# One dependent chain for the 31 taps of a depthwise convolution, in a two-layer decoder step on one Trainium2 core

## The chip, the cores and the metric

The kernel runs on one core of a Trainium2 chip. The metric is the device time of one execution, in microseconds (us); lower is better. The core's engines run side by side and meet only at semaphores: TensorE (PE in the profile) multiplies matrices, VectorE (DVE) and ScalarE (ACT) work element by element and can read and write PSUM, GpSimd (POOL) works element by element in SBUF, SyncE (SP) issues most of the DMAs.

## The reference

Two layers over a residual stream of width 2048. A prompt of 1024 rows and 64 sample rows (8 sequences of 8) share the weights. Layer 0 is the part that the change touches:

```python
def conv_mixer(u, buf, w_in, conv_w, conv_b, ln_g, ln_b, w_out):
    z = u @ w_in
    a, b, gate = jnp.split(z, 3, axis=-1)
    c = a * jax.nn.sigmoid(b)
    full = jnp.concatenate([buf, c], axis=1)          # 30 earlier rows, then c
    y = depthwise_conv(full, conv_w)                  # 31 taps for each of 2048 features
    y = y + conv_b
    y = jax.nn.silu(layer_norm(y, ln_g, ln_b))
    out = (y * jax.nn.silu(gate)) @ w_out
```

For the prompt the 30 earlier rows are zeros; the samples bring theirs in `state_conv`. Layer 1 is a sliding-window attention with a gate. Each layer is `h = h + rms_norm(mixer(rms_norm(h)))`. All is float32.

## The kernel before, in words

Features lie on the 128 partitions, the 1088 rows (1024 of the prompt, 64 of the samples) on the free axis. A weight tile `n` gives 128 output features: PE goes over 16 slices `k` of the inputs and three column chunks of 364, 364 and 360, with three matmuls each, since weights and activations are held as a high and a low part (`w_hi`, `w_lo`, `u_hi`, `u_lo`). Tiles with an even number go to the PSUM tensor `z_even`, the odd ones to `z_odd`. For each quarter of a weight tile SP loads `w_raw`, ACT makes `w_hi` (L734, `split_w`), POOL makes `w_lo` (L1021, `rest_w`), and PE waits for it.

The convolution stage is a loop over 16 feature tiles `j`. Tile `2j` is the sigmoid's half, tile `2j+1` the other. For each `j`:

- DVE reads `z_odd` (L1302 to L1307), multiplied with the sigmoid, into `cp` (1024 prompt columns behind 30 zeros) and `cs` (samples).
- ACT writes tap 0 with the convolution's bias into `aux1` (L778), a PSUM tensor of two banks, and signals `tap0_ready`.
- DVE adds the other taps. Each is one `scalar_tensor_tensor` over 128x1024: a shifted window of `cp`, times one column of `cols`, plus the accumulator. After tap 15 it reads the next `z_even` (L1269, `read_z`).
- DVE signals `conv_ready`; ACT reads `aux1` out (`read_conv`, L762 to L765: a copy and a square), and after that, in its program order, makes the last quarter of a `w_hi` (L734) and the next tap 0 (L778).
- POOL adds the two results to the layer norm's sums (`add_y`, L1071 and L1072), and does the samples' whole convolution (L1094, L1102, L1106) between the first two and the last two quarters of `w_lo` of tile `2j+3`.

`j` = 0 and `j` = 15 are written out with constants; `j` = 1 to 14 are a hardware loop on DVE, where the value that a wait compares with, and the address of the tap's column in `cols`, are worked out by register instructions on the engine's queue (DVEq, and ACTq for ACT). In the program each tap has its wait on `tap` first and the instruction with its column's address behind it.

After `j` = 15 PE sums the layer norm's totals (L562) and goes on with gates, output projection, keys and values, attention and the last projection, none of which the change touches.

The accumulators before are two: `aux1` for the even taps, and `odd_taps` in SBUF for the odd ones. A tap waits only for the one two places back (`i - 2`), the one that last wrote its accumulator. `aux1` and `odd_taps` are added at the end (L1324).

Of the kernel before, what the change touches and what calls it, by code (L numbers as in the profile page):

```python
# [31 lines left out]
ALU = mybir.AluOpType  # L32
# [6 lines left out]
TP = 1024  # L39
SB, SS = 8, 8  # L40
TS = SB * SS
T = TP + TS
# [4 lines left out]
CW = 31  # L47
HIST = CW - 1
SEG = HIST + SS
# [11 lines left out]
C_CW = 128  # L61
# [28 lines left out]
def trunk_kernel(nc, x_t, state_t, ck_t, cv, w, cols_in, y_t, scp_t, ckp_t, cvp, scs_t, cks_t, cvs):  # L90
    ctx = ExitStack()
    with ctx:
        def sb(name, shape, dt=F32):
            return ctx.enter_context(nc.sbuf_tensor(name, shape, dt))

        def sem(name):
            return ctx.enter_context(nc.semaphore(name))
# [15 lines left out]
        cols = sb("cols", [P, NCOLS])  # L113
# [11 lines left out]
        aux1 = aux[:, :, :].rearrange("p a b -> p (a b)")  # L125

        def region(at, n):
            return work[:, at:at + n]

        def places(*sizes):  # L130
            out, at = [], 0
            for n in sizes:
                out.append(region(at, n))
                at += n
            assert at <= WORK, at
            return out


        (r_a, sig, y_st, y_sq, acc_y, acc_y2, cp, cs_flat, ys, prod, odd_taps) = places(
            T, T, T, T, T, T, TP + 32, SB * SEG, TS, 4 * SS * CW, TP)  # L140
        cs = cs_flat.rearrange("p (b s) -> p b s", b=SB)

        s_st = [region(8 * T, T), region(9 * T, T), region(T, T), region(3 * T, T)]
# [81 lines left out]
        conv_ready = sem("conv_ready")  # L225
        tap = sem("tap")
# [51 lines left out]
        def ge(eng, s, v):  # L278

            if not (isinstance(v, int) and v <= 0):  # L280
                eng.wait_ge(s, v)

        def chunk(ap, c):
            return ap[:, CHUNKS[c][0]:CHUNKS[c][0] + CHUNKS[c][1]]
# [962 lines left out]
        def _(dve):  # L1247
# [17 lines left out]
            def read_z(n, z, out, by):  # L1265

                dve.wait_ge(w_used, NQ * (n + 1))
                for c in range(3):
                    ins = dve.tensor_tensor(chunk(out, c), z[:, c, 0:CHUNKS[c][1]], chunk(by, c), ALU.mult)  # L1269
                ins.then_inc(z_read, 1)  # L1270
# [8 lines left out]
            for k in range(KT):  # L1279
                dve.wait_ge(u_hi_ready, k + 1)  # L1280
                dve.scalar_tensor_tensor(out=u_lo[:, k, :], in0=x_st[k % 4],
                                         scalar=cols[:, C_PRE0 + k:C_PRE0 + k + 1],
                                         in1=u_hi[:, k, :].bitcast(F32), op0=ALU.mult, op1=ALU.subtract
# [10 lines left out]
            def glu(j, nxt):  # L1294

                dve.wait_ge(w_used, NQ * (2 * j + 2))
                dve.wait_ge(sigr_ready, j + 1)
                ge(dve, ys_ready, j)
                ge(dve, state_out, 32 * j)
                ge(dve, conv_ready, j)  # L1300
                n0, n1 = CHUNKS[0][1], CHUNKS[1][1]
                dve.tensor_tensor(cp[:, HIST:HIST + n0], z_odd[:, 0, 0:n0], chunk(sig, 0), ALU.mult)  # L1302
                dve.tensor_tensor(cp[:, HIST + n0:HIST + n0 + n1], z_odd[:, 1, 0:n1], chunk(sig, 1), ALU.mult)
                left = TP - n0 - n1
                dve.tensor_tensor(cp[:, HIST + n0 + n1:HIST + TP], z_odd[:, 2, 0:left],
                                  sig[:, n0 + n1:TP], ALU.mult)
                dve.tensor_tensor(cs[:, :, HIST:SEG], z_odd[:, 2, left:left + TS].rearrange("p (b t) -> p b t", b=SB),  # L1307
                                  sig[:, TP:T].rearrange("p (b t) -> p b t", b=SB), ALU.mult).then_inc(z_read, 1)

                dve.wait_ge(z_read, 2 * j + 2)  # L1310
                dve.tensor_scalar(odd_taps, cp[:, 1:1 + TP], cols[:, bass.ds(C_CW + j * CW + 1, 1)], None,
                                  ALU.mult).then_inc(tap, 1)
                dve.wait_ge(tap0_ready, j + 1)
                for i in range(2, CW):
                    if i > 2:
                        dve.wait_ge(tap, (CW - 1) * j + i - 2)
                    acc = odd_taps if i % 2 else aux1
                    dve.scalar_tensor_tensor(out=acc, in0=cp[:, i:i + TP],  # L1318
                                             scalar=cols[:, bass.ds(C_CW + j * CW + i, 1)], in1=acc,
                                             op0=ALU.mult, op1=ALU.add).then_inc(tap, 1)  # L1320
                    if i == CW // 2 and nxt:
                        read_z(2 * j + 2, z_even, sig, r_a)
                dve.wait_ge(tap, (CW - 1) * j + CW - 1)
                dve.tensor_tensor(aux1, aux1, odd_taps, ALU.add).then_inc(conv_ready, 1)  # L1324

            glu(0, True)
            with dve.Fori(1, KT - 1) as j:
                glu(j, True)
            glu(KT - 1, False)


# [263 lines left out]
```

## Time and profile before

| | |
|---|---|
| median of 3 runs | 3283.92 us (3283.34 to 3286.16) |
| the profiled execution | 3287.02 us |
| its span in the trace | 3285.4 us |
| PE busy | 3081.3 us, 94% |
| DVE busy | 1505.7 us, 46% |
| POOL busy | 1551.2 us, 47% |
| ACT busy | 850.7 us, 26% |

Busy shares are means over the whole span. The convolution's loop takes the stretch from about 83 to 897 us, and there DVE is busy nearly all the time, while elsewhere it is busy for a third of the time or less. So what the change is worth has to be read from that stretch.

### The profile page before, as it was taken

The numbers are of one execution on the slowest core, as the hardware profiler recorded it, in microseconds if no ns is written. First come the engines' busy times: TensorE is split into PE (matmuls) and PEld (weight loads), VectorE is DVE, ScalarE is ACT, GpSimd is POOL, SyncE is SP. The second block draws the span as 40 slices with busy tenths as digits, with TensorE's granted clock in tenths as the row PEclk, the third lists the DMA queues.
The fourth block names the chain that finished last, engine by engine and source line by source line (L and its number), as shares of the span: only waits on it lengthen the run. The fifth ranks groups of instructions, "written<-read, shape, count | busy, mean of one in ns | idle before, by whom it ended". The sixth has DMA issues, their size and how long they took to land.

```text
span 3285.4 us, 50429 instructions
## 1 busy us (share of the span) xinstructions
PE 3081.3 (94%) x19117; PEld 2965.2 (90%) x19117; DVE 1505.7 (46%) x1729; ACT 850.7 (26%) x1708; POOL 1551.2 (47%) x1153
## 2 busy tenths in 40 slices
PE   6999999999899999999968999999999999899995
PEld 6999999999889999999948899899899889799985
DVE  6999999999931114000092234433433442500043
ACT  5121111211221224121231223222322222422332
POOL 2778778787733334333344233333333333244475
PEclk9999999999999999999989999999999999899997
DMA  5121221211122225121273211211211211422386
GB/s 163 41 71 50 57 59 47 71 50 57 56 96 94 81 95 178 66 69 67 82 275 101 57 48 42 58 48 42 58 45 47 58 39 51 157 91 90 106 293 213
DMA packets 171678, 284.87 MB, mean 87 GB/s; under 512 B 62009, under 2 KB 72505, under 8 KB 171577
## 3 DMA queue, kind: packets, MB, share of 16 engines
q1 hardware_dynamic: 127328, 222.48, 22.3%
q10 hardware_dynamic: 41912, 52.32, 4.4%
q0 software_dynamic: 2352, 8.88, 0.7%
q8 instruction: 61, 1.00, 0.1%
q14 instruction: 25, 0.20, 0.0%
HBM read 218.44 MB, written 67.15 MB: 87 GB/s over the span
## 4 chain that ended last, share of the span: by engine, by line
PE 47%; issue 20%; DVE 14%; POOL 10%; ACT 5%; DMA 3%; ACTq 1%; DVEq 0%; SPq 0%; POOLq 0%
PE z_even L512 8%; PE z_even L513 8%; PE z_even L515 8%; PE z_odd L512 7%; PE z_odd L513 7%; PE z_odd L515 7%; POOL w_lo L1021 4%; DVE aux L1318 2%; DMA work<-conv_scratch 2%; ACT work L939 1%; POOL work L1102 1%; DVE work L1318 1%; DVE work L1414 1%; POOL work L1130 1%; DVE work L1417 1%
## 5 line engine op out<-in xcount | busy, mean ns | idle before, releaser
L1021 POOL TENSOR_TENSOR w_lo<-w_raw,w_hi 128x512 fp32r<-128x512 f32 x528 | 747.7, 1424 | 1372.6 <-ACT w_hi L734 1372.0
L512 PE MATMUL z_even<-u_hi,w_hi 128*128 128x364 f32 (+1 forms) x2784 | 924.8, 332 | 86.6 <-POOL u_lo L1182 33.7
L512 PE MATMUL z_odd<-u_hi,w_hi 128*128 128x364 f32 (+1 forms) x2784 | 940.8, 338 | 63.1 <-POOL w_lo L1021 63.1
L513 PE MATMUL z_odd<-u_lo,w_hi 128*128 128x364 f32 (+1 forms) x2784 | 924.3, 332 | 0.0
L513 PE MATMUL z_even<-u_lo,w_hi 128*128 128x364 f32 (+1 forms) x2784 | 920.6, 331 | 0.0
L734 ACT ACTIVATE w_hi<-w_raw 128x512 fp32r<-128x512 f32 x528 | 331.3, 630 | 1687.1 <-PE z_even L515 813.5
L515 PE MATMUL z_odd<-u_hi,w_lo 128*128 128x364 f32 (+1 forms) x2784 | 638.1, 331 | 0.0
L515 PE MATMUL z_even<-u_hi,w_lo 128*128 128x364 f32 (+1 forms) x2784 | 634.8, 329 | 0.0
L512 PEld LDWEIGHTS z_even<-u_hi,w_hi 128*128 128x128 f32 x2784 | 529.2, 190 | 105.7 <-issue 36.8
L512 PEld LDWEIGHTS z_odd<-u_hi,w_hi 128*128 128x128 f32 x2784 | 533.0, 191 | 101.1 <-POOL w_lo L1021 58.9
L513 PEld LDWEIGHTS z_odd<-u_lo,w_hi 128*128 128x128 f32 x2784 | 533.4, 192 | 0.1
L513 PEld LDWEIGHTS z_even<-u_lo,w_hi 128*128 128x128 f32 x2784 | 529.9, 190 | 0.4 <-issue 0.3
L515 PEld LDWEIGHTS z_odd<-u_hi,w_lo 128*128 128x128 f32 x2784 | 489.4, 191 | 0.0
L515 PEld LDWEIGHTS z_even<-u_hi,w_lo 128*128 128x128 f32 x2784 | 486.2, 189 | 0.0
L1318 DVE SCALAR_TENSOR_TENSOR work<-work,cols 128x1024 f32<-128x1024 f32 x224 | 421.8, 1883 | 0.0
L1318 DVE SCALAR_TENSOR_TENSOR aux<-work,cols,aux 128x1024 f32<-128x1024 f32 x240 | 306.4, 1277 | 38.7 <-ACT aux L778 38.5
L1259 DVE TENSOR_SCALAR work<-z_even 128x364 f32<-128x364 f32 (+1 forms) x6 | 2.9, 530 | 657.5 <-PE z_even L540 657.5
L1269 DVE TENSOR_TENSOR work<-z_even,work 128x364 f32<-128x364 f32 (+1 forms) x126 | 59.4, 525 | 505.1 <-PE z_even L515 505.1
L1102 POOL TENSOR_TENSOR work<-work 128x480 f32<-128x480 f32 (+3 forms) x128 | 152.4, 1191 | 10.0
L1013 POOL TENSOR_TENSOR w_raw<-w_raw,cols 128x512 f32<-128x512 f32 x144 | 148.3, 1040 | 15.3 <-DMA branch_scratch<-work 15.3
L1094 POOL TENSOR_TENSOR work<-work,cols 128x248 f32<-128x248 f32 x128 | 130.3, 1048 | 2.9 <-POOL work L1106 2.9
L1130 POOL TENSOR_TENSOR work<-work 128x1088 f32<-128x1088 f32 x16 | 42.5, 2658 | 155.0 <-ACT work L799 141.7
(149 smaller groups left out, 2193.6 us busy)
## 6 DMA issues: line engine op xcount, KB each, us to landing
w_raw<-in_w SPq DMA_DIRECT2D x528, 256.0 KB, 2.6
work<-in_x SPq DMA_DIRECT2D x32, 544.0 KB, 5.2
work<-branch_scratch SPq DMA_DIRECT2D x31, 544.0 KB, 5.4
conv_scratch<-work ACTq DMA_DIRECT2D x16, 544.0 KB, 2.7
work<-conv_scratch SPq DMA_DIRECT2D x16, 544.0 KB, 3.9
resid_scratch<-work ACTq DMA_DIRECT2D x16, 544.0 KB, 5.4
branch_scratch<-work ACTq DMA_DIRECT2D x16, 512.0 KB, 2.6
branch_scratch<-work POOLq DMA_DIRECT2D x15, 544.0 KB, 3.0
```

The costliest lines, as they stand in the source:

```text
L512: pe.matmul(o, w_hi[:, q, at:at + P], chunk(u_hi[:, k, :], c), start=(i == 0), stop=False)
L513: pe.matmul(o, w_hi[:, q, at:at + P], chunk(u_lo[:, k, :], c), start=False, stop=False)
L515: mm = pe.matmul(z[:, c, 0:CHUNKS[c][1]], w_lo[:, q, at:at + P], chunk(u_hi[:, k, :], c), start=False, stop=(i == KT - 1))
L734: act.activation(w_hi[:, q, :], w_raw[:, q, :], ACT.Copy).then_inc(w_hi_ready, 1)
L939: ins = act.activation(sc[u][:, i, :], sc[u][:, i, :], ACT.Exp, scale=HD ** -0.5, bias=st[:, 4 + i:5 + i], accum_out=st[:, 16 + i:17 + i])
L1013: pool.tensor_tensor(w_raw[:, q, :].rearrange("p (k c) -> p k c", k=4), w_raw[:, q, :].rearrange("p (k c) -> p k c", k=4), cols[:, gain + ...
L1021: pool.tensor_tensor(w_lo[:, q, :], w_raw[:, q, :], w_hi[:, q, :].bitcast(F32), ALU.subtract).then_inc(w_lo_ready, 1)
L1094: ins = pool.tensor_tensor(pr[:, b], win, cols[:, bass.ds(C_CW + j * CW, CW)].unsqueeze(1).to_broadcast([P, SS, CW]), ALU.mult)
L1102: pool.tensor_tensor(pm[:, :, 0:m], pm[:, :, 0:m], pm[:, :, other:other + m], ALU.add).then_inc(pool_step, 1)
L1130: pool.tensor_tensor(s_st0, yb0[par], gg0[par], ALU.mult).then_inc(s_ready, 1)
L1269: ins = dve.tensor_tensor(chunk(out, c), z[:, c, 0:CHUNKS[c][1]], chunk(by, c), ALU.mult)
L1318: dve.scalar_tensor_tensor(out=acc, in0=cp[:, i:i + TP], scalar=cols[:, bass.ds(C_CW + j * CW + i, 1)], in1=acc, op0=ALU.mult, op1=ALU.add ...
```

## The change

All taps of the prompt go into `aux1`. The buffer `odd_taps` goes, with the first odd tap's `tensor_scalar` (L1311) and the final addition (L1324). Tap 1 is now an addition to `aux1` too, behind `tap0_ready`. Each later tap waits for the tap right before it. The last tap signals `conv_ready` itself.

```diff
-                dve.tensor_scalar(odd_taps, cp[:, 1:1 + TP], cols[:, bass.ds(C_CW + j * CW + 1, 1)], None,
-                                  ALU.mult).then_inc(tap, 1)
                 dve.wait_ge(tap0_ready, j + 1)
-                for i in range(2, CW):
-                    if i > 2:
-                        dve.wait_ge(tap, (CW - 1) * j + i - 2)
-                    acc = odd_taps if i % 2 else aux1
-                    dve.scalar_tensor_tensor(out=acc, in0=cp[:, i:i + TP],
-                                             scalar=cols[:, bass.ds(C_CW + j * CW + i, 1)], in1=acc,
-                                             op0=ALU.mult, op1=ALU.add).then_inc(tap, 1)
+                for i in range(1, CW):
+                    if i > 1:
+                        dve.wait_ge(tap, (CW - 2) * j + i - 1)
+                    dve.scalar_tensor_tensor(out=aux1, in0=cp[:, i:i + TP],
+                                             scalar=cols[:, bass.ds(C_CW + j * CW + i, 1)], in1=aux1,
+                                             op0=ALU.mult, op1=ALU.add
+                                             ).then_inc(conv_ready if i == CW - 1 else tap, 1)
                     if i == CW // 2 and nxt:
                         read_z(2 * j + 2, z_even, sig, r_a)
-                dve.wait_ge(tap, (CW - 1) * j + CW - 1)
-                dve.tensor_tensor(aux1, aux1, odd_taps, ALU.add).then_inc(conv_ready, 1)
```

## Rows read from the trace of the kernel before

**Rows 1.** Windows: start:end, us, busy us (count) by engine, then PEclk, DMA.

```profile
440.00:491.00 51.00, 51.00 (x311) 51.00 (x310) 48.11 (x39) 9.69 (x14) 40.42 (x29) 1.00 0.21 57
491.00:543.00 52.00, 48.60 (x279) 48.30 (x279) 49.01 (x39) 9.69 (x14) 39.36 (x29) 0.93 0.22 56
```

**Rows 2.** Waits from 90 to 950 us: total us, times, longest.

```profile
ACT work L762 <- DVE aux L1324: 126.7, 16, 9.8
...
PE z_odd L512 <- POOL w_lo L1021: 39.3, 13, 4.9
```

**Rows 3.** Groups by line and shape, 90 to 900 us: the taps.

```profile
L1318 DVE SCALAR_TENSOR_TENSOR work<-work,cols 128x1024 f32<-128x1024 f32 x223 | 420.5, 1886 | 0.0
L1318 DVE SCALAR_TENSOR_TENSOR aux<-work,cols,aux 128x1024 f32<-128x1024 f32 x238 | 303.9, 1277 | 38.5 <-ACT aux L778 38.5
```

**Rows 4.** Timeline of DVE, 440 to 560 us: taps 15 to 30, next iteration's start.

```profile
465.15 1.36 DVE L1318 SCALAR_TENSOR_TENSOR work<-work,cols 128x1024 f32<-128x1024 f32 x1
466.43 1.41 DVE L1269 TENSOR_TENSOR work<-z_even,work 128x364 f32<-128x364 f32 x3
467.76 1.27 DVE L1318 SCALAR_TENSOR_TENSOR aux<-work,cols,aux 128x1024 f32<-128x1024 f32 x1
...
488.88 1.28 DVE L1318 SCALAR_TENSOR_TENSOR aux<-work,cols,aux 128x1024 f32<-128x1024 f32 x1
490.19 1.23 DVE L1324 TENSOR_TENSOR aux<-aux,work 128x1024 f32<-128x1024 f32 x1
491.53 0.54 DVE L1302 TENSOR_TENSOR work<-z_odd,work 128x364 f32<-128x364 f32 x1
...
493.18 0.75 DVE L1311 TENSOR_SCALAR work<-work,cols 128x1024 f32<-128x1024 f32 x1 [0.16 <-DVE work L1307]
496.53 1.29 DVE L1318 SCALAR_TENSOR_TENSOR aux<-work,cols,aux 128x1024 f32<-128x1024 f32 x1 [2.59 <-ACT aux L778]
```

**Rows 5.** Chain of waits in order of time, 438 to 450 us: start, us, what.

```profile
440.06 0.04 ACTq L281
...
440.13 0.04 ACTq L281
...
440.21 0.07 ACT work L762
...
444.98 0.03 issue
445.01 0.06 DVEq L1318
445.07 0.05 issue
```

**Rows 6.** Timeline of DVE, iterations 0, 1 and 15 (the last).

```profile
85.91 1.29 DVE L1318 SCALAR_TENSOR_TENSOR aux<-work,cols,aux 128x1024 f32<-128x1024 f32 x1
...
106.94 1.42 DVE L1269 TENSOR_TENSOR work<-z_even,work 128x364 f32<-128x364 f32 x3 [2.91 <-PE z_even L515]
...
132.87 0.54 DVE L1302 TENSOR_TENSOR work<-z_odd,work 128x364 f32<-128x364 f32 x1
...
849.66 0.54 DVE L1302 TENSOR_TENSOR work<-z_odd,work 128x364 f32<-128x364 f32 x1
...
895.94 1.23 DVE L1324 TENSOR_TENSOR aux<-aux,work 128x1024 f32<-128x1024 f32 x1
```

**Rows 7.** Timeline of PE: first matmuls of tiles 3 and 4, a stall, the layer norm's sums.

```profile
106.74 0.33 PE L512 MATMUL z_odd<-u_hi,w_hi 128*128 128x364 f32 x1
...
130.53 0.33 PE L512 MATMUL z_even<-u_hi,w_hi 128*128 128x364 f32 x1
...
526.27 0.67 PE L512 MATMUL z_odd<-u_hi,w_hi 128*128 128x364 f32 x1 [3.40 <-POOL w_lo L1021]
...
540.71 0.33 PE L512 MATMUL z_even<-u_hi,w_hi 128*128 128x364 f32 x1
...
904.66 1.58 PE L562 MATMUL aux<-work,ones 128*128 128x364 f32 x2 [4.96 <-POOL work L1072]
```

More of the change, by code:

```diff
@@ L136, in places @@
             return out
-        (r_a, sig, y_st, y_sq, acc_y, acc_y2, cp, cs_flat, ys, prod, odd_taps) = places(
-            T, T, T, T, T, T, TP + 32, SB * SEG, TS, 4 * SS * CW, TP)
+        (r_a, sig, y_st, y_sq, acc_y, acc_y2, cp, cs_flat, ys, prod) = places(
+            T, T, T, T, T, T, TP + 32, SB * SEG, TS, 4 * SS * CW)
         cs = cs_flat.rearrange("p (b s) -> p b s", b=SB)
```

## The prediction

> **What bounds the kernel now.** The page's shares say PE, at 94%. They are a mean over stages, so I looked next at the windows of single iterations of the convolution loop [rows 1]. DVE is busy for 48 to 49 us of each, POOL for 40, ACT for 10. PE shows 51.00 of 51.00 in one and 48.60 of 52.00 in the next, at a granted clock of 0.93: it stalls now and then, and each stall also costs clock. The waits name both sides [rows 2]. PE waited 39.3 us in all for `w_lo`, and ACT waited 126.7 us for DVE's last addition. Free of stalls a PE tile takes 130.53 - 106.74 = 23.79 us [rows 7], two tiles 47.6 us. The loop runs slower than that: the reads of `z_odd` of j = 1 and j = 15 stand at 132.87 and 849.66 us [rows 6], 14 periods of 51.20 us.
>
> What closes the ring is seen in the timeline of DVE [rows 4]. L1324 ends at 490.19 + 1.23 = 491.42. DVE is then held until 496.53, with 2.59 us idle behind L778: ACT has to read `aux1` out before it writes the next tap 0 into it. These 5.11 us and the taps make up the period. The ring is DVE's taps, ACT's read-out, ACT's tap 0. POOL and PE follow it. That PE isn't the leader shows in tile `2j+3`: `w_lo` arrives 526.27 - 491.42 = 34.9 us after `conv_ready`, and the tile ends near 540.8, before DVE's next read of `z_odd` at about 542.7 (491.53 + 51.2) [rows 4, 7]. At the stage's end PE stands still for POOL's L1072 and starts the layer norm's sums at 904.66, 7.5 us after the last L1324 ended (895.94 + 1.23 = 897.17) [rows 6, 7]. So time saved on the taps moves the end one for one, until PE's 47.6 us per iteration become the ring.
>
> **The taps' durations.** Into SBUF a tap takes 1886 ns in the mean, into PSUM 1277 ns [rows 3]. The single rows of taps into PSUM all lie at 1.27 to 1.29 [rows 4, 6]; the one into SBUF at 465.15 lasts 1.36, so the mean of 1886 hides much longer ones. I read this as DVE and POOL getting in each other's way when a tap has both tensors in SBUF. The change makes all 30 the steady kind. (The Trainium skill, "SBUF — State Buffer", the section on the sides that share nothing but the port pair, says that a DVE instruction with two SBUF inputs and a GpSimd one exclude each other for a whole instruction. By that rule, the trace agrees, POOL's own work shortens as well; the sum below takes nothing for it.)
>
> **The price of the dependence.** Two taps that don't wait for each other start 1.19 us apart, 0.08 us less than one lasts: tap 15 of 1.36 us is followed after 1.28 [rows 4]. A dependent pair stands there too: the last tap starts at 488.88, L1324, which reads its result, at 490.19, a pitch of 1.31. But L1324 has no register instruction between its wait and itself. A tap in the hardware loop has one, for its column's address, behind the wait. The chain of waits shows what follows [rows 5]: ACT's tap 0 ends at 444.98; 0.03 us later the 0.06 us register instruction runs; 0.05 us later the tap starts. That is 0.14 us after the end it waited for. L1311, the same build behind L1307, started 0.16 us after it [rows 4]. So the pitch in the loop is 1.277 + 0.14 = 1.42 us. In j = 0 and j = 15, with constants, it is 1.31.
>
> From below, the pitch can't be under 1.19 (no wait felt) and is likely not under 1.31. From above, ACT's L762, with two register instructions behind its wait, started 0.19 to 0.20 us after DVE's end [rows 4, 5], which would make 1.47. I take 1.42, since the instruction sequence is the same as in the row.
>
> (The Trainium skill, "VectorE: DVE Perf Modes", section "The DRAIN you can't avoid", states that a semaphore after every operation costs nothing against one after the last. The rows disagree with 0.12 us for each; were it right, the case is the first rival below, with its time.)
>
> **The sum.** For j = 1 to 14, from one `conv_ready` to the next:
> - to the first tap: 5.11 us, as before. L1311 falls away but stood inside this wait, and tap 1 takes the place in line that tap 2 had. ACT's read-out, the last `w_hi` quarter and tap 0 are unchanged.
> - 30 taps have 29 pitches. One of them holds the read of `z_even`: 1.19 to its start (a read doesn't wait for the tap), and 467.76 - 466.43 = 1.33 to the next tap [rows 4], by when the wait for tap 15 is long over: 2.52 us. The other 28 take 28 x 1.42 = 39.8.
> - the last tap lasts 1.28. L1324's 1.23 is gone.
>
> Sum 5.11 + 39.8 + 2.52 + 1.28 = 48.7 (48.5 with 1.416). I carry 48.6, against 51.20: 2.6 us less. That is 1.0 us above PE's 47.6, so DVE's ring still leads.
>
> j = 0: first tap at 85.91 as now. Tap 15 ends at 85.91 + 14 x 1.31 + 1.28 = 105.5, the read still waits for PE at 106.94 [rows 6], then 1.33 + 14 x 1.31 + 1.28 end the chain at 127.9. Now PE is late: tile 3 ends at 130.7 [rows 7]. The read of `z_odd` starts at 130.8 in place of 132.87, takes 1.6 us (as 491.53 to 493.1), ACT's tap 0 takes an estimated 1.3 (DVE's pass over as many columns lasts 1.28), and tap 1 starts 0.14 later at 133.8. Iteration 1 then ends at 133.8 + 43.5 = 177.3. From there the ring loses 1.0 us to PE in each iteration, so PE is soon ahead, and a tile up to 5.11 - 3.0 = 2.1 us late would cost nothing, since `z_odd` is read while ACT reads `aux1` out. Iterations 2 to 14 take 13 x 48.6 = 631.8, to 809.1. j = 15: 5.0 to the first tap, 29 x 1.31 + 1.28 = 39.3, with no read inside: 853.4. Before it was 897.17. The gain is 43.8 us.
>
> PE needs tile 33 done before the sums: at its free rate 130.7 + 30 x 23.79 = 844.4, and by POOL's 34.9 us, half a tile of 11.9 and 2.5 us of lost clock (540.71 - 526.27 - 11.9 [rows 7]) at 809.1 + 49.3 = 858.4. The sums start at 853.4 + 7.5 = 860.9, so this stays hidden even if POOL gains nothing. Behind 904.66 nothing is touched; I let it shift whole. 3287.0 - 43.8 = 3243.2 for an execution like the profiled one. That one lies 3.1 us above the median of the runs, so the median should be 3283.9 - 43.8, about **3240 us**. What a measurement of this kernel can tell from no change is about 0.2%, 6.6 us.
>
> **The rivals.**
> - *PE becomes the ring.* If a dependent tap costs a pitch of 1.31 in the loop too (the register instruction hides), DVE's ring is 5.11 + 36.7 + 3.80 = 45.6, under PE's 47.6. Then `z_odd` of j = 15 is ready at 130.7 + 28 x 23.79 = 796.8, tap 1 starts 3.0 later, the chain ends at 839.1 and the sums start at 846.6, 58 us early: 3226. For it speaks the L1324 row; against it that L1324 has no address to work out. Nothing in it goes faster still, as tile 33 ends at 844.4.
> - *Two register instructions behind each wait.* The loop also has one for the wait's own value. If it falls behind the end of the tap before, the pitch is 1.47, the ring 50.1, and the gain 43.8 - 14 x 1.4 = 24: 3260. Against it: it stands ahead of the wait in the program and would run under the tap.
> - *No change.* If the ring went through POOL and PE and the taps had slack, 3284. The 126.7 us of ACT behind L1324 [rows 2] speak against it.
> - *Slower.* The dependence costs more than 0.24 us a tap in PSUM, say because an accumulator written and read again at once has to wait for its write. The ring is 8.9 + 28 x pitch; it equals 51.20 at 1.51. Counting the 5 us that the first and last iterations save, the break-even is near 1.52. At 1.55 the loop is 52.3, 14 x 1.1 = 15 longer, less 5: 3294. Against it: L1324 reads the accumulator right behind its write, in PSUM, and started 0.03 us after the tap's end.
>
> **How the numbers follow.** The forecast has 0.74, PE as the ring 0.12, two register instructions 0.07, no change 0.03, slower 0.04. Faster by over 0.2% is the sum of the first three, 0.93. The range takes in the neighbours: down to 3225 for the PE-bound case, up to 3260 for a pitch of 1.47. The forecast's own range is 3233 to 3250 (pitch 1.40 to 1.44, 28 x 14 x 0.02 = 8 us each way).
>
> **What would show it.** In the profile after: no L1318 row with a mean over 1.29 us; taps in the loop 1.42 us apart and 1.31 in the last iteration; reads of `z_odd` 48.6 us apart; ACT's read-out still waiting for DVE, for less; PE's wait for `w_lo` well under 39.3 us and POOL's busy time below 40 in each iteration; the last `conv_ready` near 853 and the layer norm's sums near 861. The prediction is wrong if the pitch isn't 1.42, if the 5.11 us grow, say because ACT's `w_hi` quarter waits for a later PE, or if the stages behind lose what this one gains.

## The result and the profile after

The changed kernel takes 3249.05 us (median of 4 runs, 3247.18 to 3253.61); beside it the kernel before took 3285.04 us (4 runs). The ratio is 0.9892, with a 95% interval of 0.9875 to 0.9909: 36.0 us less. Predicted were 3240 us and 43.8 us less. The profiled execution took 3247.58 us, its span is 3246.0.

Two windows of one iteration each, the columns as in [rows 1]:

```profile
450.00:499.00 49.00, 49.00 (x299) 49.00 (x298) 41.26 (x38) 9.56 (x14) 28.82 (x30) 1.00 0.21 60
499.00:548.00 49.00, 48.24 (x292) 47.89 (x291) 41.26 (x38) 9.56 (x14) 28.78 (x30) 1.00 0.21 60
```

POOL was busy for 39 to 40 us of an iteration [rows 1] and is now for 29, with the same work. DVE fell from 48 or 49 to 41, though an iteration still takes 49: the rest is idle time, between the taps and ahead of tap 1.

The groups by line and shape, 90 to 900 us, answer to [rows 3]; the last three are POOL's:

```profile
L1315 DVE SCALAR_TENSOR_TENSOR aux<-work,cols,aux 128x1024 f32<-128x1024 f32 x478 | 616.1, 1289 | 109.7 <-ACT aux L778 51.1 <-DVE aux L1315 0.3
...
L1021 POOL TENSOR_TENSOR w_lo<-w_raw,w_hi 128x512 fp32r<-128x512 f32 x128 | 163.6, 1295 | 276.8 <-ACT w_hi L734 276.7
...
L1094 POOL TENSOR_TENSOR work<-work,cols 128x248 f32<-128x248 f32 x128 | 83.7, 689 | 2.9 <-POOL work L1106 2.9
...
L1072 POOL TENSOR_TENSOR work<-work 128x1088 f32<-128x1088 f32 x16 | 40.7, 2543 | 0.0
```

All taps are of one kind now, 1289 ns, which is 12 ns more than a tap into `aux1` had. POOL's three groups took 1732, 1048 and 3528 ns in the mean before. The rest of what a tap costs stands in the idle time and, for one tap after another, in the chain of waits (start, us, what):

```profile
528.83 1.30 DVE aux L1315
530.13 0.03 issue
530.16 0.06 DVEq L1315
530.22 0.05 issue
530.27 1.30 DVE aux L1315
```

A tap, 0.03 us, the register instruction, 0.05 us, the next tap: a pitch (from start to start) of 1.43 to 1.44 us. The timeline of DVE shows one whole iteration:

```profile
500.87 21.35 DVE L1315 SCALAR_TENSOR_TENSOR aux<-work,cols,aux 128x1024 f32<-128x1024 f32 x15
522.32 0.54 DVE L1302 TENSOR_TENSOR work<-z_odd,work 128x364 f32<-128x364 f32 x1
...
527.40 21.36 DVE L1315 SCALAR_TENSOR_TENSOR aux<-work,cols,aux 128x1024 f32<-128x1024 f32 x15 [3.59 <-ACT aux L778]
548.67 1.41 DVE L1269 TENSOR_TENSOR work<-z_even,work 128x364 f32<-128x364 f32 x3
550.00 9.88 DVE L1315 SCALAR_TENSOR_TENSOR aux<-work,cols,aux 128x1024 f32<-128x1024 f32 x7
```

Fifteen taps take 21.35 us, so the pitch is (21.35 - 1.29) / 14 = 1.433. The last one ends at 522.22 and the first of the next iteration starts 5.18 later, at 527.40. The first and last reads of `z_odd` behind the first iteration, and DVE's last taps, which end at 839.28 + 22.49 = 861.77:

```profile
131.34 0.54 DVE L1302 TENSOR_TENSOR work<-z_odd,work 128x364 f32<-128x364 f32 x1 [2.96 <-PE z_odd L515]
...
817.12 0.54 DVE L1302 TENSOR_TENSOR work<-z_odd,work 128x364 f32<-128x364 f32 x1
...
839.28 22.49 DVE L1315 SCALAR_TENSOR_TENSOR aux<-work,cols,aux 128x1024 f32<-128x1024 f32 x17
```

14 periods take 817.12 - 131.34 = 685.8 us, 48.98 each; an undisturbed one takes 28 x 1.433 + 5.18 + 1.20 + 1.33 + 1.29 = 49.1. The mean is lower because in iteration 1, where DVE had waited for PE, the first tap came 2.97 us after the read of `z_odd` began, and not some 5.1. PE's timeline has the rows that answer to [rows 7], and the waits those to [rows 2]:

```profile
548.59 0.43 PE L512 MATMUL z_odd<-u_hi,w_hi 128*128 128x364 f32 x1 [1.36 <-POOL w_lo L1021]
...
869.25 0.97 PE L562 MATMUL aux<-work,ones 128*128 128x364 f32 x1 [13.79 <-POOL work L1072]
```

```profile
ACT work L762 <- DVE aux L1315: 196.3, 16, 16.2
...
DVE aux L1315 <- ACT aux L778: 51.1, 15, 3.6
...
PE z_odd L512 <- POOL w_lo L1021: 12.3, 8, 3.3
```

The sums start at 869.25 in place of 904.66: 35.4 us early, which is the median's gain. `w_lo` for the third quarter is there 548.59 - 522.22 = 26.4 us after `conv_ready`, where it took 34.9, and PE's stalls shrank to 12.3 us. ACT waits longer for DVE than before, 196.3 us in place of 126.7 [rows 2]. In the same views its `w_hi` quarters waited 141.4 us for the DMA of `w_raw` before and 13.0 now, so ACT reaches the read-out earlier. The profiled pair of executions differs by 39.4 us; the 4 us beyond the sums' shift come later, in stages that the change doesn't touch. The shift is 35.4 us at the sums, 33.0 near 1610 us (the first L540) and 39.4 at the end, and executions of one kernel differ by 4 to 6 us.

### The profile page after: what moved, and what is told of

It reads as the page before. It is cut to its first block, busy times and chain, and to the rows that moved or that the text cites. A ratio compares the mean times of both kernels' runs of the same rounds, so it can differ in the third digit from the quotient of the medians.

```text
span 3246.0 us, 50429 instructions
## 1 busy us (share of the span) xinstructions
PE 3064.6 (94%) x19117; PEld 2950.8 (91%) x19117; DVE 1400.1 (43%) x1713; ACT 849.3 (26%) x1708; POOL 1372.1 (42%) x1153
## 4 chain that ended last, share of the span: by engine, by line
PE 56%; DVE 28%; issue 7%; ACT 5%; POOL 2%; DMA 1%; DVEq 1%; ACTq 1%; SPq 0%; POOLq 0%
DVE aux L1315 17%; PE z_even L512 9%; PE z_even L513 9%; PE z_even L515 9%; PE z_odd L512 8%; PE z_odd L513 8%; PE z_odd L515 8%; ACT work L939 1%; DVE work L1410 1%; DVE work L1413 1%; POOL w_lo L1021 1%; DVE work L1416 1%; PE z_even L627 1%; DVE work L1388 1%; DVEq L1315 1%
## 5 line engine op out<-in xcount | busy, mean ns | idle before, releaser
L1021 POOL TENSOR_TENSOR w_lo<-w_raw,w_hi 128x512 fp32r<-128x512 f32 x528 | 691.4, 1318 | 1483.0 <-ACT w_hi L734 1482.5
L1315 DVE SCALAR_TENSOR_TENSOR aux<-work,cols,aux 128x1024 f32<-128x1024 f32 x480 | 618.7, 1289 | 111.1 <-ACT aux L778 52.5
L512 PEld LDWEIGHTS z_odd<-u_hi,w_hi 128*128 128x128 f32 x2784 | 525.9, 189 | 66.6 <-issue 42.1
L513 PEld LDWEIGHTS z_odd<-u_lo,w_hi 128*128 128x128 f32 x2784 | 526.8, 189 | 0.1
L939 ACT ACTIVATE work<-work 128x128 f32<-128x128 f32 x272 | 104.9, 387 | 0.0
L1269 DVE TENSOR_TENSOR work<-z_odd,work 128x364 f32<-128x364 f32 (+1 forms) x78 | 36.9, 529 | 148.7 <-PE z_odd L515 148.5
L1159 POOL TENSOR_TENSOR work<-work 128x1088 f32<-128x1088 f32 (+2 forms) x45 | 84.9, 1886 | 24.1 <-ACT work L854 24.0
```

Of the source, the lines that this page charges most:

```text
L512: pe.matmul(o, w_hi[:, q, at:at + P], chunk(u_hi[:, k, :], c), start=(i == 0), stop=False)
L513: pe.matmul(o, w_hi[:, q, at:at + P], chunk(u_lo[:, k, :], c), start=False, stop=False)
L939: ins = act.activation(sc[u][:, i, :], sc[u][:, i, :], ACT.Exp, scale=HD ** -0.5, bias=st[:, 4 + i:5 + i], accum_out=st[:, 16 + i:17 + i])
L1021: pool.tensor_tensor(w_lo[:, q, :], w_raw[:, q, :], w_hi[:, q, :].bitcast(F32), ALU.subtract).then_inc(w_lo_ready, 1)
L1159: pool.tensor_tensor(acc_o[:, t0:t1], acc_o[:, t0:t1], sq_o[par][:, t0:t1], ALU.add).then_inc(o_added, 1)
L1315: dve.scalar_tensor_tensor(out=aux1, in0=cp[:, i:i + TP], scalar=cols[:, bass.ds(C_CW + j * CW + i, 1)], in1=aux1, op0=ALU.mult, op1=ALU.a ...
```

## The experiments

Seven kernels ran, all on one chip. Beside the first four the kernel before took 3287.07 us, beside the other three, later, 3286.25. The ratios below are to those. Experiments 3, 4 and 5 are single runs; their differences are far above the 4 to 6 us by which executions of one kernel differ.

**1. The tap columns at a fixed place.** Is the gap behind each wait the register instruction, and is DVE's ring the bound?

```diff
+                dve.tensor_copy(tapw[:, :], cols[:, bass.ds(C_CW + j * CW, CW)]).then_inc(tapw_ready, 1)
+                dve.wait_ge(tapw_ready, j + 1)
                 dve.wait_ge(tap0_ready, j + 1)
...
-                                             scalar=cols[:, bass.ds(C_CW + j * CW + i, 1)], in1=aux1,
+                                             scalar=tapw[:, i:i + 1], in1=aux1,
```

> The changed kernel, but the 31 columns of an iteration are copied once to a fixed place, so that no tap has an address to work out behind its wait. Theory (DVE's ring of taps is the bound, and 0.11 us of each tap's 0.135 us gap is the register instruction): pitch 1.32 us in the loop too, DVE's ring 5.18 + 28 x 1.32 + 2.53 + 1.29 = 46.0 us, under PE's 47.6, so PE becomes the bound; the layer norm's sums start near 847 us in place of 869 and the time is near 3227 us. Rival (the gap is the semaphore's, whatever stands behind it): pitch stays 1.43 and the time 3249 us. Rival (POOL or PE is the bound of the changed kernel already): pitch 1.32, but the time stays 3249.

Measured: 3227.05 us (5 runs, 3224.18 to 3231.19), ratio 0.9817, 0.9804 to 0.9831. The timeline of DVE in this kernel:

```profile
439.20 1.29 DVE L1319 SCALAR_TENSOR_TENSOR aux<-work,tapw,aux 128x1024 f32<-128x1024 f32 x1
441.07 1.42 DVE L1271 TENSOR_TENSOR work<-z_even,work 128x364 f32<-128x364 f32 x3 [0.58 <-PE z_even L517]
442.41 19.83 DVE L1319 SCALAR_TENSOR_TENSOR aux<-work,tapw,aux 128x1024 f32<-128x1024 f32 x15
465.18 0.54 DVE L1304 TENSOR_TENSOR work<-z_odd,work 128x364 f32<-128x364 f32 x1 [2.94 <-PE z_odd L517]
...
488.65 1.42 DVE L1271 TENSOR_TENSOR work<-z_even,work 128x364 f32<-128x364 f32 x3 [0.58 <-PE z_even L517]
```

Fifteen taps take 19.83 us: a pitch of 1.324, 0.11 less than in the changed kernel. The columns' copy, with its wait, is the only thing added. DVE now waits for PE at both reads, and an iteration takes 488.65 - 441.07 = 47.58 us, PE's two tiles. Both rivals fall. The time is within 1 us of the one that the prediction gave for PE as the ring, 3226.

**2. Two halves of the columns.** The wait is kept, but put two instructions back.

```diff
                 for i in range(1, CW):
-                    if i > 1:
-                        dve.wait_ge(tap, (CW - 2) * j + i - 1)
+                    for half in range(2):
+                        if i > 1:
+                            dve.wait_ge(tap, 2 * (CW - 2) * j + 2 * (i - 2) + half + 1)
+                        at = 512 * half
```

The instruction inside works on `aux1[:, at:at + 512]`, and `conv_ready` counts both halves.

> The changed kernel, but each tap is two instructions of 512 columns, one for each bank of the accumulator; each waits for its own half's tap before, which is two instructions back. Theory (what the change pays for is the exposed wait, not the place): the waits and register instructions hide under the other half; a half should take about 0.66 us from start to start, a tap 1.32, and the time falls to PE's bound near 3227 us. Rival (the fixed part of an instruction is larger than the wait it hides): a tap takes 1.5 us or more, and the time is 3280 us or more.

Measured: 3226.1 us (4 runs, 3221.75 to 3227.74), ratio 0.9812, 0.9797 to 0.9827. The timeline of DVE:

```profile
441.00 19.85 DVE L1317 SCALAR_TENSOR_TENSOR aux<-work,cols,aux 128x512 f32<-128x512 f32 x30
463.77 0.54 DVE L1302 TENSOR_TENSOR work<-z_odd,work 128x364 f32<-128x364 f32 x1 [2.92 <-PE z_odd L515]
```

Thirty halves of 0.75 us start (19.85 - 0.75) / 29 = 0.659 us apart, a tap takes 1.32. Here each instruction still has its register instruction and its wait; both run under the other half. So it is their exposure that costs: with every tap still in PSUM and every address still worked out, the time is that of experiment 1.

**3. The dependence alone.** The kernel before, with its two accumulators.

```diff
-                        dve.wait_ge(tap, (CW - 1) * j + i - 2)
+                        dve.wait_ge(tap, (CW - 1) * j + i - 1)
```

> The kernel before with its two accumulators, but each tap waits for the tap right before it. This is the dependence alone, without the change of place. Theory: each of 29 taps starts 0.135 us after the end of the one before in place of 0.08 us ahead of it, 0.22 us x 29 = 6.2 us an iteration in the loop, 3.5 us in the first and last: near 3285 + 94 = 3379 us. Rival (DVE's taps have slack behind POOL and PE): under 3300 us.

Measured: 3338.85 us in one run, 52 us over the kernel before. The groups by line, 90 to 1000 us:

```profile
L1318 DVE SCALAR_TENSOR_TENSOR work<-work,cols 128x1024 f32<-128x1024 f32 x223 | 380.9, 1708 | 29.3 <-DVE aux L1318 0.2
L1318 DVE SCALAR_TENSOR_TENSOR aux<-work,cols,aux 128x1024 f32<-128x1024 f32 x238 | 306.6, 1288 | 67.8 <-ACT aux L778 38.6 <-DVE work L1318 3.9
```

The sign is the theory's, the size is not: 52 us where 94 were expected. The taps into SBUF became shorter, 1708 ns for 1886 [rows 3]. 223 x 0.178 = 40 us, which is nearly the difference of 42; the expectation had held their duration fixed. A likely reason is that taps spaced further apart meet POOL less often; no run tests it by itself. The 12 ns on the taps into `aux` are here too, with the places as before, so they don't come with the place.

**4. The place alone.** The changed kernel's one chain, in SBUF.

```diff
-                    dve.scalar_tensor_tensor(out=aux1, in0=cp[:, i:i + TP],
-                                             scalar=cols[:, bass.ds(C_CW + j * CW + i, 1)], in1=aux1,
+                    dve.scalar_tensor_tensor(out=acc_s, in0=cp[:, i:i + TP],
+                                             scalar=cols[:, bass.ds(C_CW + j * CW + i, 1)], in1=acc_s,
```

ACT writes tap 0 to `acc_s` and reads it out of there.

> The changed kernel with its one chain, but the accumulator is in SBUF. This is the place alone. Theory (taps with both tensors in SBUF and POOL's instructions hold each other up): taps of 1.28 to 3.6 us, 1.6 to 1.9 in the mean, an iteration of 58 to 66 us, 3376 to 3490 us in all. Rival (the place doesn't matter, the old kernel's long taps had another cause): 1.29 us a tap and 3249 us.

Measured: 3500.59 us in one run, 252 us over the changed kernel, a little above the range expected. The groups by line of DVE, 90 to 1000 us, the taps' line by itself, the waits from 90 to 1050 us, and POOL's products:

```profile
L1315 DVE SCALAR_TENSOR_TENSOR work<-work,cols 128x1024 f32<-128x1024 f32 x422 | 765.6, 1814 | 105.8 <-ACT work L778 51.6 <-DVE work L1315 0.5
```

```profile
L1315 DVE SCALAR_TENSOR_TENSOR work<-work,cols x480: 1273/1490/3600, 86.1 to 1107.3; 128x1024 f32<-128x1024 f32 x160
```

```profile
PE z_odd L512 <- POOL w_lo L1021: 213.6, 15, 15.3
```

```profile
L1094 POOL TENSOR_TENSOR work<-work,cols x128: 662/1662/1717, 97.4 to 1084.0; 128x248 f32<-128x248 f32 x128
```

The same 480 instructions with the same waits take 1273 to 3600 ns in place of a steady 1289. The harm goes both ways: one of POOL's products takes 1662 ns in the median, 687 in the changed kernel, and PE then waits 214 us for `w_lo`.

**5. POOL's load taken away from the kernel before.**

```diff
-                            pr[:, b], win,
-                            cols[:, bass.ds(C_CW + j * CW, CW)].unsqueeze(1).to_broadcast([P, SS, CW]), ALU.mult)
+                            pr[:, b, :, 0:1], win[:, :, 0:1],
+                            cols[:, bass.ds(C_CW + j * CW, 1)].unsqueeze(1).to_broadcast([P, SS, 1]), ALU.mult)
```

The additions behind it work on one column as well.

> The kernel before, with nearly all of the samples' convolution left out: POOL's instructions for it are issued, but each on one tap's width only, so the samples' outputs are not those of the reference. Theory (the long taps into SBUF are collisions with POOL): POOL's 18 to 20 us an iteration of them go, about half of its work beside the taps, and the mean of the taps into SBUF falls from 1.89 to 1.6 us or less; the ring falls by about 4.5 us to the neighbourhood of PE's 47.6, and the time to 3230 to 3245 us. Rival (the taps into SBUF are slow by themselves): 1.89 us and 3287 us.

Measured: 3231.49 us in one run. The groups by line of DVE, 90 to 850 us:

```profile
L1318 DVE SCALAR_TENSOR_TENSOR work<-work,cols 128x1024 f32<-128x1024 f32 x223 | 349.1, 1565 | 0.0
L1318 DVE SCALAR_TENSOR_TENSOR aux<-work,cols,aux 128x1024 f32<-128x1024 f32 x239 | 305.6, 1279 | 12.2 <-ACT aux L778 12.2
```

Nothing of DVE's was changed, and its taps into SBUF fell from 1886 to 1565 ns, while those into PSUM stayed as they were. So the samples' instructions on POOL cause 0.32 us of the 0.61 by which a tap into SBUF was longer than one into PSUM. The rest stayed, as did POOL's `w_lo` and its additions. DVE now waited for PE at every read of `z_odd` (47.8 us in 16 waits), so PE's rate sets this time.

Single rows from the timelines of DVE and POOL in the kernel before, 440 to 560 us, show who held up whom:

```profile
462.76 1.27 DVE L1318 SCALAR_TENSOR_TENSOR work<-work,cols 128x1024 f32<-128x1024 f32 x1
462.92 1.29 POOL L1102 TENSOR_TENSOR work<-work 128x64 f32<-128x64 f32 x1
...
477.07 2.55 POOL L1077 TENSOR_TENSOR work<-work 128x1088 f32<-128x1088 f32 x1
477.08 3.62 DVE L1318 SCALAR_TENSOR_TENSOR work<-work,cols 128x1024 f32<-128x1024 f32 x1
...
487.69 1.27 DVE L1318 SCALAR_TENSOR_TENSOR work<-work,cols 128x1024 f32<-128x1024 f32 x1
...
495.36 1.30 POOL L1021 TENSOR_TENSOR w_lo<-w_raw,w_hi 128x512 fp32r<-128x512 f32 x1 [10.02 <-ACT w_hi L734]
```

The tap at 462.76 came first: it took 1.27 us, and POOL's small addition, begun inside it, took 1.29, where its mean in the changed kernel is 0.32. At 477.07 POOL's addition came first: it took 2.55, and the tap beside it 3.62, nearly the sum of the two. The tap at 487.69 fell into POOL's idle 10.02 us and took 1.27.

**6 and 7. ACT's last quarter behind tap 0**, in the changed kernel and in that of experiment 1.

```diff
-                split_w(2 * j + 2, 3)
                 act.wait_ge(z_read, 2 * j + 2)
                 act.activation(aux1, cp[:, 0:TP], ACT.Identity, scale=cols[:, bass.ds(C_CW + j * CW, 1)],
                                bias=cols[:, bass.ds(C_CB + j, 1)]).then_inc(tap0_ready, 1)
+                split_w(2 * j + 2, 3)
```

> The changed kernel, with ACT's last w_hi quarter of tile 2j+2 moved from ahead of tap 0 to behind it. Theory (the ring of the changed kernel is DVE's taps and ACT's steps from conv_ready to tap 0): the wait from conv_ready to the first tap falls from 5.18 to about 4.6 us, an iteration from 49.1 to 48.5, and the time by 15 x 0.6 = 9 us, to 3240 us. Rival (PE or POOL sets the pace): 3249 us, as PE gets its last quarter a little later, at worst some us more.

Measured: 3245.4 us (4 runs, 3244.7 to 3247.33), ratio 0.9879, 0.9863 to 0.9894. The intervals of this ratio and of the changed kernel's overlap, so the traces have to tell. The timeline of ACT, 440 to 505 us, that of DVE, and the quarter's row in the changed kernel:

```profile
474.04 0.34 ACT L765 ACTIVATE work<-work,cols 128x64 f32<-128x64 f32 x1
474.54 0.34 ACTq L767 DMA_DIRECT2D conv_scratch<-work  x1
475.21 1.21 ACT L777 ACTIVATE aux<-work,cols 128x1024 f32<-128x1024 f32 x1 [0.82 <-ACT work L765]
```

```profile
423.07 0.54 DVE L1302 TENSOR_TENSOR work<-z_odd,work 128x364 f32<-128x364 f32 x1
...
471.89 0.54 DVE L1302 TENSOR_TENSOR work<-z_odd,work 128x364 f32<-128x364 f32 x1
```

```profile
525.44 0.63 ACT L734 ACTIVATE w_hi<-w_raw 128x512 fp32r<-128x512 f32 x1 [0.62 <-ACT work L765]
```

An iteration takes 48.82 us in place of 49.13: 0.31 less, half of the 0.6 expected. In the changed kernel the quarter started after 0.62 us of idle time behind ACT's last step (L765), and tap 0 started 0.54 after the quarter, at 525.98. Now tap 0 starts after 0.82 us of idle time behind that step. So the quarter had added 0.54 us and covered 0.20 of what tap 0 needs on the queue; 0.34 is left, near the 0.31 of the period. The direction supports that ACT's steps are in the ring; that the median's 3.6 us are more than noise is carried by the period and by the layer norm's sums, which start at 865.5 in place of 869.25, not by the medians.

> The kernel with the tap columns at a fixed place, and ACT's last w_hi quarter behind tap 0 as well. Theory (with fixed columns PE's 47.6 us per iteration are the bound in the convolution): nothing more is won, 3227 us, within 3 us; only the last iteration's chain, 0.6 us shorter, may show. Rival (DVE's ring still leads there): 3218 us.

Measured: 3228.45 us (5 runs, 3226.05 to 3232.13), ratio 0.9826, 0.9813 to 0.9840, against 3227.05 and 0.9817 for experiment 1. An iteration takes 47.57 us, from one read of `z_even` to the next. Nothing more is won: PE is the bound there.

## Why the prediction was right, and where it was off

**The ring.** Right. The sums' start moved by what the taps saved (35.4 us; the last tap's end moved from 897.17 to 861.77), experiment 6 shortened the period by a step of ACT's, and experiments 1 and 2 brought the period down to PE's 47.6 us and no further.

**The place.** Right, and more than was claimed: experiment 5 shows POOL as a cause of the long taps, and its single rows the holding up in both directions; experiment 4 shows what the place is worth to one chain. That POOL's work shortens too was left out of the sum. No effect of it on the time is seen, since PE's third quarter was not on the ring; it shows in PE's stalls and in `w_lo` arriving 8.5 us sooner. This is the exclusive lock that the Trainium skill states in "SBUF — State Buffer", section "SBUF: two separate sides": whichever starts first has the shared ports for its whole instruction. The trace agrees: the tap behind POOL's addition took 3.62 us, POOL's small addition behind a tap 1.29 for 0.32.

**The dependence.** The mechanism and its two parts were right: the lost overlap and the exposed register instruction. The gap behind a tap's end was forecast at 0.14 us, and the chain of waits shows 0.03 + 0.06 + 0.05. Experiment 1 takes the register instruction's 0.11 away and leaves 1.324. Instructions that don't wait for one another started 1.19 us apart (487.69 and 488.88), dependent ones 1.32 without an address to work out, 1.43 with one. The Trainium skill states in "VectorE: DVE Perf Modes", section "The DRAIN you can't avoid", that a semaphore after each operation costs nothing extra. Read as one on waits, as the prediction read it, this does not hold here. For the signal alone the trace doesn't speak against it: in the kernel before each tap signals too, and starts 1.19 us after the one before.

**The size.** The sums started at 869.25, not near 860.9. The term that was off is the sum of an iteration, "Sum 5.11 + 39.8 + 2.52 + 1.28 = 48.7 (48.5 with 1.416). I carry 48.6"; 49.13 were measured. The tap's duration of 1.277 is the mean of taps of which nearly all start while DVE is still at work on the one before; in the new chain they last 1.289. So the pitch was 1.433, not 1.42, which is 28 x 0.013 = 0.36 us; 0.1 is from carrying 48.6 for 48.7 (the alternative in brackets is 48.56, not 48.5), and 0.07 from 5.18 for 5.11. Over 14 iterations this is 7.4 us of the 8.3. The other 0.9 us lie in the last iteration (39.72 us of taps for 39.3) and at the start, where the read of `z_odd` came at 131.34 in place of 130.8, with PE some 0.3 us later than in the trace before.

The row at 439.20 in experiment 1, and the 1288 ns of experiment 3, show that the 12 ns come without the register instruction and without the change of place. Nor does it take a dependence on another tap: in the kernel before, the first tap of an iteration waits for ACT alone and lasts 1.29 [rows 4, 6]. In the changed kernel tap 16, which starts at 451.74 while the read before it still runs, lasts 1.280, and the next one 1.290. So the long value goes with starting on a DVE that has run dry, and the row at 496.53 [rows 4] had shown it beforehand; 1.289 + 0.144 is the measured pitch. Why such a tap lasts longer was not settled.

**What was forecast to stay hidden, stayed hidden.** PE's last tile ended 13.8 us ahead of the sums, and the stages behind them shifted as a whole within the spread of executions.

**The signs.** One came out the other way: ACT's wait for DVE was to shrink and grew, from 126.7 to 196.3 us. ACT was off the ring until `conv_ready`, so the time does not show it. The others came in kind, if not in size: no tap's mean is over 1.29 us, POOL is busy for 29 us of an iteration, PE's wait for `w_lo` is 12.3 us, the reads of `z_odd` are 49.1 us apart for 48.6, and the last `conv_ready` and the sums came 8 us later than forecast, which leaves a gain of 36.0 us for the 43.8.

**A better version.** Fixed tap columns (3227 us) or two halves (3226 us) beat both kernels, by about 22 us against the changed one and 60 against the one before. They end at PE's rate, so a further gain in this stage would have to come from PE.

## What to carry to other kernels

A chain of dependent instructions pays for all that stands between the wait and the instruction, register instructions for addresses included. Look for that in the chain of waits before choosing how many accumulators to have, and take the addresses out of the loop or let a second, independent instruction cover them. Take the duration of one link from a row that itself started behind a wait, not from a mean over instructions that overlap. Where an elementwise instruction's durations scatter and another with one operand in PSUM does not, look at what GpSimd runs at the same time: moving one operand into PSUM can be worth more than the parallelism that is given up for it.

## What was not expected

- A tap that starts on an idle DVE lasts 1289 ns in the profile, one that starts while the instruction before still runs 1272 to 1280.
- Taps into SBUF got shorter when each was started some 0.2 us later: 1886 ns fell to 1708. So an added wait cost 52 us where 94 were worked out.
- POOL gained more from the change than DVE's taps had lost to it. Its busy time in an iteration fell by 11 us (its samples' products from 1048 to 689 ns in the mean), where the 14 taps into SBUF had been longer than the others by 14 x 0.61 = 8.5 us.
